# Two-layer mixture-of-experts block with a recurrent block behind it: where and how the twelve modulation vectors are computed, and how semaphores are cleared

## What is computed

```python
c_act = jax.nn.silu(c)
for l in range(DEPTH):                       # DEPTH = 2
    mod = c_act @ w_ada[l] + b_ada[l]        # w_ada[l]: 1024 x 6144, f32
    shift1, scale1, gate1, shift2, scale2, gate2 = split(mod, 6)
    h = rms_norm(x, norm1_g[l]) * (1.0 + scale1) + shift1
    ...                                      # projections, attention, convolution
    mix = concat(attn_out, conv_out) @ w_out[l]
    x = x + gate1 * mix
    h2 = rms_norm(x, norm2_g[l]) * (1.0 + scale2) + shift2
    x = x + gate2 * expert_choice_ffn(h2, w_router[l], w_gate[l], w_up[l], w_down[l])
```

## Time and profile before

| what | us |
|---|---|
| median of 3 runs (3975.6 to 3978.51) | 3977.16 |
| the profiled execution, whole | 3975.68 |
| its span | 3973.9 |
| setup, until the next stage's first matmul | 175.0 |
| output projection, layer 0 | 624 to 738 |
| output projection, layer 1 | about 1880 to 1994 |
| PE busy, share of the span | 89% |
| DVE busy | 62% |

### The profile page before, as it was taken

How to read it: one execution, slowest core, us unless ns; L and a number is a source line. 1 busy time by engine, 2 the same in 40 slices (tenths; PEclk the granted TensorE clock), 3 DMA queues, 4 the chain that set the end, 5 groups by cost and what they waited for, 6 DMA issues and landing times. The chain is left out here.

```text
span 3973.9 us, 47220 instructions
## 1 busy us (share of the span) xinstructions
PE 3517.1 (89%) x16392; PEld 2800.9 (70%) x16392; DVE 2466.7 (62%) x2229; ACT 1648.8 (41%) x1644; POOL 1170.1 (29%) x688
## 2 busy tenths in 40 slices
PE   4798798779999969879949999969998789999998
PEld 1375597558888757378728888857877678888886
DVE  7787775478888769777358888865118431212124
ACT  5521443258888630244227888843115110000101
POOL 0142233311111124133321111104542535453632
PEclk9899899889999979989969999989998889999999
DMA  9610001469999720000049999952100211111111
GB/s 339 242 38 18 10 14 38 164 242 395 395 395 396 299 77 32 14 15 20 32 186 358 394 393 395 394 203 95 48 29 0 85 38 58 53 42 53 43 52 53
DMA packets 143147, 610.67 MB, mean 154 GB/s; under 512 B 16480, under 2 KB 34272, under 8 KB 93920
## 3 DMA queue, kind: packets, MB, share of 16 engines
q1 hardware_dynamic: 133856, 576.21, 37.7%
q0 software_dynamic: 9216, 33.56, 3.3%
HBM read 563.06 MB, written 41.94 MB: 152 GB/s over the span
## 5 line engine op out<-in xcount | busy, mean ns | idle before, releaser
L1630 DVE TENSOR_TENSOR ex_lo<-ex_raw,ex_hi 128x2048 fp32r<-128x2048 f32 x378 | 858.5, 2291 | 115.6 <-ACT ex_hi L1580 115.0
L1580 ACT CAST ex_hi<-ex_raw 128x2048 fp32r<-128x2048 f32 x378 | 720.7, 1914 | 139.6 <-PE psum L1542 139.6
L1540 PE MATMUL psum<-ex_hi,xe_hi 128*128 128x512 f32 x1024 | 404.1, 395 | 1.3 <-DVE xe_lo L1635 1.3
L1542 PE MATMUL psum<-ex_hi,xe_lo 128*128 128x512 f32 x1024 | 400.7, 391 | 0.0
L1541 PE MATMUL psum<-ex_lo,xe_hi 128*128 128x512 f32 x1024 | 400.3, 391 | 0.0
L516 DVE SCALAR_TENSOR_TENSOR mix<-y,lcols,mix 128x1024 f32<-128x1024 f32 x176 | 278.8, 1585 | 5.7
L2399 DVE TENSOR_TENSOR ff_full<-psum,ff_full 128x1024 f32<-128x1024 f32 x22 | 26.9, 1225 | 408.4 <-PE psum L431 408.4
L416 POOL TENSOR_SCALAR up_hi<-up_raw 128x1024 fp32r<-128x1024 f32 x44 | 122.1, 2776 | 361.6 <-PE psum L431 337.6
L431 PE MATMUL psum<-hn_hi,up_hi 128*128 128x512 f32 x704 | 218.2, 391 | 5.3 <-DVE hn_lo L1753 5.2
L1540 PEld LDWEIGHTS psum<-ex_hi,xe_hi 128*128 128x128 f32 x1024 | 193.4, 189 | 40.9 <-issue 2.1
L1542 PEld LDWEIGHTS psum<-ex_hi,xe_lo 128*128 128x128 f32 x1024 | 193.2, 189 | 40.7
(11 more groups left out here) (404 smaller groups left out, 7748.6 us busy)
## 6 DMA issues: line engine op xcount, KB each, us to landing
ex_raw<-w_experts_dram SPq DMA_DIRECT2D x384, 1024.0 KB, 7.6
ada_w<-w_ada_dram SPq DMA_DIRECT2D x24, 2048.0 KB, 11.6
up_raw<-w_gate_up_dram SPq DMA_DIRECT2D x44, 512.0 KB, 3.3
in_raw<-w_in_dram SPq DMA_DIRECT2D x24, 512.0 KB, 3.4
p_raw<-w_in_dram SPq DMA_DIRECT2D x24, 512.0 KB, 3.4
wd_raw<-w_down_dram SPq DMA_DIRECT2D x11, 1024.0 KB, 5.4
lo_raw<-w_out_dram SPq DMA_DIRECT2D x16, 512.0 KB, 3.3
moe_rows<-zero_row SPq DMA_DIRECT2D x16, 512.0 KB, 4.5
```

The source lines that it names most:

```text
L1540: pe.matmul(bank(out), x_hi, h[:, k, :], start=first, stop=False)
L1542: mm = pe.matmul(bank(out), x_lo, h[:, k, :], start=False, stop=end)
L1580: act.copy(hi[j % PARTS][:], raw[j % RAW][:]).then_inc(w_hi, 1)
L1630: dve.tensor_tensor(lo[j % PARTS][:], raw[j % RAW][:], hi[j % PARTS][:].bitcast(F32), ALU.subtract).then_inc(w_lo, 1)
```

## The change

**Setup** computes only four chunks: shift1, scale1 and gate1 of layer 0 and gate1 of layer 1 (`chunks = [0, 1, 2, N_MOD + 2]`). There is no matmul over the weights any more. A chunk is a sum of eight 128 x 1024 tiles, each scaled by one column of `c_act` (`mod_product`), and eight matmuls by a column of ones then sum over the partitions and give columns (`mod_columns`). Chunks 0, 1 and 2 run on DVE; chunk 3 is scaled by ACT and added by POOL. Chunk 0 stands ahead of the squares of `x` on DVE, chunks 1 and 2 behind them. SP loads the weights as 16 pieces of 1 MB in a ring of eight, eight of them ahead of `x`.

**Output projection** gets five chunks per layer: shift2, scale2 and gate2 of its own layer, shift1 and scale1 of the next (of layer 0 after layer 1). These are 40 steps on DVE, five ahead of the first tile and five after each of the first seven tiles, and 40 loads of 512 KB on SP into a ring of four (two of these are the buffers `cn_sq`). PE runs `mod_columns` after tiles 2, 4, 5 and 7. PE's loop over the whole tiles and DVE's loop over the tiles are written out.

**Router**: `gain` for the second norm is computed at its start; PE transposes straight from `h`, POOL's eight copies are gone, and the loop is written out.

**Clears**: runs of neighbouring semaphores are cleared by one instruction. 19, 91 and 62 instructions become 1, 1 and 2.

```diff
+        def mod_product(dve, acc, w, k):
+            if k == 0:
+                return dve.tensor_scalar(acc, w, c_act[:, 0:1], None, ALU.mult)
+            return dve.scalar_tensor_tensor(out=acc, in0=w, scalar=c_act[:, k:k + 1], in1=acc, op0=ALU.mult, op1=ALU.add)
+        def mod_columns(pe, cols, acc):
+            for j in range(DT):
+                mm = pe.matmul(cols[:, j:j + 1], acc[:, j * P:(j + 1) * P], ones_col, start=True, stop=True)
+            return mm
...
+                order = [(c, n) for n in range(4) for c in (0, 3)] + [(c, n) for c in (1, 2) for n in range(4)]
...
+                        for at in range(ADA_RING):
+                            load(at)
                         sp.dma_start(x[:], A["x_t"].rearrange("(k p) s -> p k s", p=P)).then_inc(x_in, 16)
...
+                        for at in range(ADA_RING):
+                            if at % 2 == 0:
+                                sp.wait_ge(dve_used, at + 2)
+                            else:
+                                sp.wait_ge(act_used, at + 1)
+                            load(ADA_RING + at)
...
+                        for k in range(1, DT):
+                            pool.wait_ge(act_used, k + 1)
+                            if k > 1:
+                                pool.wait_ge(pool_added, k - 1)
+                            pool.tensor_tensor(acc[3][:], acc[3][:], prod[k % 2][:], ALU.add).then_inc(pool_added, 1)
```

And in `conv_norm_and_mix`:

```diff
+                        load_tile(0)
+                        load_tile(1)
+                        load_ada(0, 2)
+                        load_tile(2)
+                        load_tile(3)
+                        sp.wait_ge(added, CT - 1)
+                        load_ada(2, 9)
+                        for n in range(4, DT):
+                            load_tile(n)
+                            load_ada(5 * (n - 4) + 9, 5 * (n - 4) + 14)
+                        load_ada(29, n_steps)
...
+                            for c in {2: (0,), 4: (1,), 5: (2,), 7: (3, 4)}.get(n, ()):
+                                pe.wait_ge(ada_used, (c + 1) * DT)
+                                mod_columns(pe, mod_psum[:, c * DT:(c + 1) * DT], mod_acc[c % 2]).then_inc(reduced, 1)
...
-                        add_to_x(dve, w["done"], w["read"], gate, (x_sq, x_sq_done, x_sq_added))
+                        mod_steps(0, 5)
+                        for n in range(DT):
+                            dve.wait_ge(w["done"][n % 2], n // 2 + 2)
+                            ...
+                            add_square(n)
+                            if n < DT - 1:
+                                mod_steps(5 * n + 5, 5 * n + 10)
```

More of the change, by code:

```diff
@@ L57 @@
 N_MOD = 6
[L58 to L59 removed]
+ADA_RING = 8
+LATE_RING = 4
+LATE_CHUNKS = 5
 CHUNK = 32
@@ L143, in _ @@
                     def _(pool):
-                        for name in sem_names:
-                            if name in ("ex_gathered", "ex_scattered") and name not in before:
+                        own = sorted(sem_names[name].num for name in sem_names if name not in before)
+                        for name in ("ex_gathered", "ex_scattered"):
+                            if name in sem_names and name not in before:
                                 pool.dma_reset(range(sem_names[name].num, sem_names[name].num + 1))
-                            if name not in before:
-                                pool.sem_clear(sem_names[name])
+                        first = 0
+                        for at in range(1, len(own) + 1):
+                            if at == len(own) or own[at] != own[at - 1] + 1:
+                                pool.sem_clear(range(own[first], own[at - 1] + 1))
+                                first = at
             sem_home[0] = home
@@ L202, in setup @@
[L202 to L211, removed]
+                ada_w = [sb(f"ada_w{i}", [P, 2, D], F32, ctx) for i in range(ADA_RING)]
@@ L1078, in _, with load_tile, load_ada @@
                     def _(sp):
-                        stream_tiles(sp, lambda n: tiles(n + l * DT), w, DT // 2)
+                        def load_tile(n):
+                            if n >= 2:
+                                sp.wait_ge(w["split"][n % 2], 2 * (n // 2) + 1)
+                            sp.dma_start(w["raw"][n % 2][:], tiles(n + l * DT)).then_inc(w["loaded"][n % 2], 16)
+                        def load_ada(first, end):
+                            for q in range(first, end):
+                                if q >= LATE_RING:
+                                    sp.wait_ge(ada_used, q - LATE_RING + 1)
+                                chunk, k = divmod(q, DT)
+                                row = (l * N_MOD + 3 + chunk if chunk < 3 else nxt * N_MOD + chunk - 3) * DT + k
+                                sp.dma_start(ring[q % LATE_RING], A["w_ada"][bass.ds(row, 1)].rearrange("a p m -> p (a m)")).then_inc(
+                                    ada_in[q % LATE_RING], 16)
+                        load_tile(0)
[9 more added lines that the diff above has]
+                        load_ada(29, n_steps)
                     @block.gpsimd
```

244 lines of the change are left out of this document (136 added, 108 removed).

## The result

| kernel | median, us | lowest to highest | ratio to before (95%) |
|---|---|---|---|
| before, beside it | 3977.84 | 3975.6 to 3981.9 | |
| after | 3882.72 | 3880.07 to 3883.73 | 0.9759 (0.9742 to 0.9776) |

The account below looks back on a forecast made before the run. Transfers were taken to fill the setup and PE to bound the output projection. 3975.7 - 97.5 (setup) - 20.4 (clears) + 19.2 (output projection) = 3877.0 us profiled, 3878 for the median; 8-in-10 range 3860 to 3902.

Parts of the forecast that it names:

- Setup: First stage: it turns from transfers to DVE, ends at 77.5 instead of 175.0 and loses 97.5 us.
- Chunk 0's end: Setup: DVE finishes chunk 0 at 46 us, 30.6 without POOL's additions, which add 16.
- The step, 1.26: Setup and output projection: one weight step on DVE takes 1.26 us, from 2.48 for two.
- Tail: End of setup: eight matmuls 1.5 us, three small additions 0.7, and 0.7 to the next stage.
- Clears: Between parts: 91 clears become 1 and 62 become 2, each 0.04 us, gaining 20.4 us over two layers.
- Output projection: This stage loses 9.6 us per layer, 19.2 for two layers, from stall, sums, late DVE and biases.
- Stall 3: Output projection, tile 2: PE waits 3 us for DVE's first addition to `x`, which stands behind five steps.
- Three sums, 4.6: Output projection: PE's sums over partitions after tiles 2, 4 and 5 cost 4.6 us per layer, unhidden.
- DVE late by 1.5: Output projection, end: DVE finishes its rounds at 743.4, 1.5 us behind PE's last tile at 741.9.
- The ring: Output projection, four load buffers: loads land in 3.3 us, DVE waits 1 us at most per round, PE loses nothing.
- The whole-length lock: Rival, output projection: POOL's splits block DVE throughout, 5.2 us a pair, 14 us more per layer, 3906; chance 0.10.
- Parts at nothing: Router, second norm's gain and written-out loops: no change in time.

Follow-up runs that it names:

- experiment 1: The kernel before with only the new range clears added; 3960.77 us against 3980.57, ratio 0.9952.
- experiment 5: The changed kernel with each of PE's sums over partitions in the output projection made twice; 3919.25 us in one execution.
- experiment 2: The changed kernel with two instead of five weight steps ahead of the first addition to `x`, later ones 5, 5, 5, 5, 6, 6, 6; 3884.24 us, ratio 0.9759.
- Experiment 4: The changed kernel with a ring of two weight buffers instead of four in the output projection; 3949.14 us in one execution.

## Why the prediction was right, step by step

**Setup**, 97.5 predicted, 93.8 measured. Start 6.3 for 7. Chunk 0's end 44.9 for 46 (my terms, 30.6 and 16.1, add up to 46.7): 0.7 by the start and 1.9 because an addition of POOL costs 2.03 and not 2.3 us, against 0.9 by longer steps. Splitting the 5.7 us of the earlier trace rows between two kinds of operation was the right idea with a wrong share: one by one, the taps there lost 2.0 us to each subtraction and 0.7 to the rounding, and the rest was the distance between taps. `x` landed at 36.5 for 38.5. Squares 10.1 for 9.2: the wait of 1.12 us for ACT stands in the earlier trace rows, and I left it out. The step, 1.26, was too short: seven in a row took 9.61, which is 1.39 from start to start. The row of 2.48 for two was of the same form, but its operation was not quite the same (ns shortest, median, longest; before, then after):

```profile
L316 DVE SCALAR_TENSOR_TENSOR table<-table x4: 1224/1224/1225, 14.3 to 21.4; 128x1024 f32<-128x1024 f32 x4
```

```profile
L198 DVE SCALAR_TENSOR_TENSOR ada_acc<-ada_w,c_act,ada_acc x21: 1283/1283/3157, 33.4 to 75.0; 128x1024 f32<-128x1024 f32 x21
L321 DVEq EVENT_SEMAPHORE  x7: 21/21/21, 55.8 to 64.1; - x7
```

The old operation has a constant as its factor and one wait, on the operation ahead of it; the next one starts 0.03 us behind its end. A weight step takes its factor from `c_act`, 1.28 us instead of 1.22, and has two waits, on the step before and on its load, for which a semaphore instruction of its own stands between steps; the gap is 0.10. That these two differences are the cause was not tried by themselves. Chunks 1 and 2 took 21.3 for 19.2. Tail: the sum took 3.57 us for the 1.5 I gave. This is the step that failed as a reading: in the earlier trace rows the 3.07 us stand beside x16, and I took eight of sixteen. A matmul of f32 leaves two records (the new sums, eight matmuls in the program, are x16 in the rows), so x16 was one sum of eight matmuls, and the row was the price of the whole. The end came at 81.2 for 77.5: 0.9 for the squares, 2.1 for the steps and 2.1 for the sum, less 1.1 at chunk 0 and 0.1 behind the sum, which is 3.9 for the 3.7 found.

**Clears**, 20.4 predicted for the four places, 18.9 found between parts; experiment 1, which has the setup's 19 clears too, gave 19.8. The price of a range was 4 to 14 times too low, and the engines wait for all of it: 2 x 0.53 for the ranges of 91 and 2 x 0.32 for those of 62 are 1.7 of the gain, for the 1.5 that are missing.

**Output projection**, 9.6 per layer predicted, 11.1 measured.
1. Stall 3: 2.93, at the place and for the reason given. The low clock behind it was in the bounds only (2.5); it cost 3.0 in tile 2, 13.9 us from its start to the sum where a tile is 10.9. It belonged into the sum: the earlier trace rows show it after 4.92 us of idleness, and here it came after 2.93, in both layers. In experiment 5, after 2.90 us of idleness at the same place in layer 0, the pairs ran in 0.62 from the second on, so it doesn't always come.
2. Three sums, 4.6: 3 x 1.84 = 5.5. The same wrong count (0.19 for a matmul) was here nearly made good by another thing: this sum ran at the full clock, the one of the earlier trace rows mostly at half. The granted clock there, and in the changed kernel at the sum of tile 2 and at the next stage's first sum:

```profile
175.00:178.00 3.00, 2.96 (x16) 3.00 (x16) 0.00 (x0) 1.28 (x1) 0.18 (x2) 0.59 0.53 135
```

```profile
590.93:592.70 1.77, 1.77 (x18) 1.77 (x16) 1.56 (x3) 0.00 (x0) 1.42 (x1) 1.00 1.04 405
...
656.40:660.00 3.60, 3.55 (x16) 3.47 (x16) 0.09 (x1) 1.11 (x2) 0.00 (x0) 0.50 0.77 263
```

The first row is of the kernel before; 1.84 us at 1.00 (2.4 GHz) and 3.55 at 0.50 (1.2 GHz) are the two prices.
3. DVE late by 1.5: it was not late. PE was 3.9 later than I had it (3.0 by the clock, 0.9 by the sums), and a pair of POOL's operations cost 2.1 and not 2.9, which over five rounds is 4 us; against it stand the longer steps and 3.2 us of one wait for a load. (My sum also took 8.6 for a round without a split, where the line before it has 8.4.) Without the stall DVE would have been the later one, as experiment 2 shows: the point that both engines are full was right.
4. The ring: landing 4.7 at the median for 3.3. DVE's waits for loads were 3.2 and twice 0.3 us in layer 0, and 2.4, 0.8 and 0.5 in layer 1. The wait of 3.2 was for a load that landed 6.4 us after its issue, so the sign that I gave for being wrong, steps that wait for landings of over 5 us, did show once there; it didn't decide, as PE was still behind. Experiment 4 has the mechanism.
In all 2.93 + 3.0 + 5.5 = 11.4 for the 11.1 found.

**The whole-length lock** would have been 5.2 per pair and 14 us more per layer; measured is 2.1 per pair. The reading behind it was right for one kind of operation. By the Trainium skill (SBUF — State Buffer, Who interferes with whom), as the prediction put it, the engine that doesn't hold the shared port fully blocks. For subtractions and additions with two inputs the runs agree nearly: 1.7 to 2.2 us lost to 2.36 or 2.39 where the operation that DVE starts next is a step or a square. Where it is an addition to `x`, that one runs on and the one behind it waits (1.0 in after). For the rounding with one input they don't: a step beside it lost 0.6 or 0.7 and ended ahead of it, others nothing.

**Parts at nothing**: the router took 72.6 us from its first load to the end of top-k where it had 73.0, and nothing outside the named places was longer.

The 4.9 us by which the profiled execution is above the sum are 3.7 in the setup, 2 x 1.5 in the output projection and 1.5 in the clears, less 3.3 in the parts taken at nothing. So part of the closeness is luck: too dear additions of POOL in the setup, and 3.3 us in parts that I had taken at nothing, made good nearly half of what was lost where the sums, the steps and the clears were priced too low and the low clock was left out. Each error sits in a small term; the large one, the transfers that no longer bound the setup, was a count of bytes and operations. How much of the 93.8 us comes from the bytes that left the setup and how much from the new arithmetic was not tried: no run has all twelve chunks with the new steps, or four with the old ones.

## What to carry to other kernels

Before a row's time is divided by its count, ask what one instruction leaves in the records and at which clock it ran; take the whole row if the new code does the same as the old line. If work is moved from a full engine under another's cover, set both engines' rounds side by side per tile: once both are full, taking away a stall of one gives no more than the distance to the other (here 2.7 of 5.9 us in one layer, 1.1 in the other). Two-input operations of POOL cost a busy DVE 1.0 to 2.2 of their 2.4 us, one-input ones 0.7 or less, so it is the former that should be kept away from it; where they can't be, an operation that reads an accumulator bank beside their start takes the smaller loss.

## What the runs showed of the hardware that was not expected

- The granted clock fell to 0.57 and 0.61 in the 4 us or so behind 3.6 us of matmuls one column wide, with PE never idle (experiment 5). Behind 1.84 us of the same the pairs of the kernel after ran at full speed all six times, but once, in experiment 2, the clock fell to 0.57 there too.
- In the setup the record of the clock stands at 1.00 while a sum takes 3.57 us, the length that it has elsewhere at 0.50. There the length tells more than the column. The stretch of after in which that sum ran:

```profile
76.30:79.90 3.60, 3.57 (x16) 3.49 (x16) 0.00 (x0) 0.00 (x0) 0.00 (x0) 1.00 0.00 0
```

- A load of 512 KB in a ring of four landed in 4.7 us at the median, in a ring of two in 3.6, and in the kernel before, with no ring beside it, in 3.3.
- POOL's subtraction held up DVE's steps and squares until its own end, but not its addition to `x` from an accumulator bank; POOL's rounding made a step 0.6 us longer or left it alone.
- The same stall of 2.9 us at the same place was followed by the half clock in one execution and by the full clock in another.
